# Fox prompt scores from two matmul passes: a stacked key and query pair, and the decay rows beside the key's low part

## The reference

```python
lk = jnp.cumsum(logf_all, axis=1)
lq = lk[:, Tk - T:]
s = jnp.einsum('bqhd,bkhd->bhqk', qi, k) * scale      # scale = 64 ** -0.5
s = s + (lq[t] - lk[s])                                # per head, per (t, s)
s = jnp.where(k_pos[None, :] <= pi[:, None], s, -jnp.inf)
p = jax.nn.softmax(s, axis=-1)
o = jnp.einsum('bhqk,bkhd->bqhd', p, v)
```

## Time and profile before

| | |
|---|---|
| median of the runs | 2846.46 us |
| span of the profiled execution | 2846.8 us |
| TensorE busy, whole span | 2649.1 us (93%) |
| VectorE, ScalarE, GpSimd busy | 938.1, 658.4, 437.9 us |
| mean granted clock of TensorE | 0.958 |
| fox, first score to last exponential | 1685.8 to 1857.7 us |

### The profile page before, as it was taken

How to read it: one execution, slowest core, us unless ns; L and a number is a source line. 1 busy time by engine, 2 the same in 40 slices (tenths; PEclk the granted TensorE clock), 3 DMA queues, 4 the chain that set the end, 5 groups by cost and what they waited for, 6 DMA issues and landing times. The chain is left out here.

```text
span 2846.8 us, 35924 instructions
## 1 busy us (share of the span) xinstructions
PE 2649.1 (93%) x14251; PEld 2340.2 (82%) x14251; DVE 938.1 (33%) x1612; ACT 658.4 (23%) x1138; POOL 437.9 (15%) x229
## 2 busy tenths in 40 slices
PE   5999999999996997889889969989899999999997
PEld 5999999999995887768745448867899999999996
DVE  4222222222226222554422254434222222222224
ACT  4111111111124011434222214433311111111112
POOL 1111111111113000000000001022111111111112
PEclk8999999999998998989989979989899999999999
DMA  4111111111014221100133030022211111111103
GB/s 152 45 44 44 44 44 44 44 44 44 15 63 156 78 80 39 38 9 0 54 116 115 31 119 0 0 94 92 81 45 44 44 44 44 36 38 44 44 15 141
DMA packets 134646, 161.61 MB, mean 57 GB/s; under 512 B 9648, under 2 KB 105008, under 8 KB 132528
## 3 DMA queue, kind: packets, MB, share of 16 engines
q1 hardware_dynamic: 134576, 160.66, 17.5%
HBM read 138.04 MB, written 22.60 MB: 56 GB/s over the span
## 5 line engine op out<-in xcount | busy, mean ns | idle before, releaser
L65 PE MATMUL ffn_gate_ps<-all_xT_hi,ffn_gu_hi 128*128 128x384 f32 x1056 | 355.8, 337 | 20.4 <-DVE all_xT_lo L163 12.2
L378 DVE TENSOR_TENSOR ffn_prod<-ffn_up_ps,ffn_silu 128x384 f32<-128x384 f32 x132 | 73.6, 558 | 893.2 <-ACT ffn_silu L346 893.2
L66 PE MATMUL ffn_gate_ps<-all_xT_lo,ffn_gu_hi 128*128 128x384 f32 x1056 | 354.9, 336 | 0.0
L67 PE MATMUL ffn_gate_ps<-all_xT_hi,ffn_gu_lo 128*128 128x384 f32 x1056 | 354.9, 336 | 0.0
L65 PE MATMUL ffn_up_ps<-all_xT_hi,ffn_gu_hi 128*128 128x384 f32 x1056 | 352.9, 334 | 0.0
L67 PE MATMUL ffn_up_ps<-all_xT_hi,ffn_gu_lo 128*128 128x384 f32 x1056 | 352.7, 334 | 0.0
L66 PE MATMUL ffn_up_ps<-all_xT_lo,ffn_gu_hi 128*128 128x384 f32 x1056 | 352.7, 334 | 0.0
L346 ACT ACTIVATE ffn_silu<-ffn_gate_ps 128x384 f32<-128x384 f32 x132 | 64.9, 492 | 1222.3 <-PE ffn_up_ps L67 1222.3
L65 PE MATMUL ffn_down_ps<-ffn_dn_hi,ffn_a_hi 128*128 128x512 f32 x792 | 309.2, 390 | 2.2 <-DVE all_acc L391 2.1
L391 DVE TENSOR_TENSOR all_acc<-ffn_down_ps,all_acc 128x512 f32<-128x512 f32 x360 | 246.0, 690 | 195.1 <-PE ffn_down_ps L67 195.1
L67 PE MATMUL ffn_down_ps<-ffn_dn_hi,ffn_a_lo 128*128 128x512 f32 x792 | 308.6, 390 | 0.0
(11 more groups left out here) (348 smaller groups left out, 3947.7 us busy)
## 6 DMA issues: line engine op xcount, KB each, us to landing
gu_raw<-in_w_ffn_gu SPq DMA_DIRECT2D x88, 512.0 KB, 5.1
ffn_dn_raw<-in_w_ffn_down SPq DMA_DIRECT2D x22, 1024.0 KB, 4.9
h<-all_acc SPq DMA_DIRECT2D x18, 512.0 KB, 2.9
dec_high_fk<-in_cache_fox_k SPq DMA_DIRECT2D x8, 1024.0 KB, 5.3
dec_x_fv<-in_cache_fox_v SPq DMA_DIRECT2D x8, 1024.0 KB, 4.7
out_fox<-inp_stage SPq DMA_DIRECT2D x27, 256.0 KB, 2.0
in_raw<-in_w_in SPq DMA_DIRECT2D x6, 1024.0 KB, 7.5
fox_x_rows<-out_fox SPq DMA_DIRECT2D x3, 2048.0 KB, 14.8
```

Of the source, the lines that this page charges most:

```text
L65: pe.matmul(out, w_hi, x_hi, start=first, stop=False)
L66: pe.matmul(out, w_hi, x_lo, start=False, stop=False)
L67: return pe.matmul(out, w_lo, x_hi, start=False, stop=last)
L378: dve.tensor_tensor(prod[:, u % 2, :], up_ps[:, u % 2, 0:GN], silu[:, u % 2, :], ALU.mult).then_inc(prod_ok, 1)
```

## The change

Only the fox stage takes it (`stacked=True`); the mla stage keeps its three passes.

- The products of the 64 head columns of high with high and high with low become one pass over 128 partitions. `k_twice` holds the key's high part twice, `q_both` holds the query's high part on partitions 0 to 63 and its low part on 64 to 127.
- The second pass is `kT_lo` against `qT_hi` on 104 partitions. kT_lo holds the key's low part and, on 64 to 75, the decay rows; qT_hi holds the high part, the low maxima on 64 to 71, the decay rows on 72 to 75 and the high maxima on 96.
- q_st and k_st are 76 wide: eight columns of zeros (q) and ones (k) at 64 leave room for the low maxima.
- ScalarE writes, for each half of k and ahead of the high part, the upper half of k_twice and the decay rows of kT_lo.
- GpSimd writes the lower halves of k_twice (an add with zero) and q_both (a copy), behind its v copy; TensorE waits for that on `doubled`. GpSimd also waits for VectorE's clearing before it stages the first head.
- VectorE clears with three memsets a buffer pair where there were five.

```diff
-        CLEARS = 2 * 2
+        doubled = k.sem("doubled")
+        CLEARS = 9 if stacked else 4
+        ROWS_CLEARED = 2 if stacked else 4
...
+                    if stacked:
+                        pool.memset(q_st[b][:, :, 64:64 + PT], 0.0).then_inc(cleared, 1)
+                        pool.memset(k_st[b][:, :, 64:64 + PT], 1.0).then_inc(cleared, 1)
+                if stacked:
+                    pool.memset(zero[:, :], 0.0).then_inc(cleared, 1)
+                    pool.wait_ge(cleared, CLEARS)
+                    pool.wait_ge(rows_cleared, 2 * ROWS_CLEARED)
...
                         pool.tensor_copy(v_st[b][:, :, 0:VD], v_of(i * 2 + b)).then_inc(v_staged, 1)
+                        for h in range(HALVES if stacked else 0):
+                            cols = slice(h * HALF, h * HALF + HALF)
+                            pool.wait_ge(prep_hi, i * (2 * PREP) + (b * PREP + 2 * h + 2))
+                            pool.tensor_tensor(k_twice[b][0:64, cols], plain(kT_hi[b][0:64, cols]), zero[0:64, :].broadcast_to([64, HALF]), ALU.add).then_inc(doubled, 1)
+                            pool.tensor_copy(q_both[b][0:64, cols], plain(qT_hi[b][0:64, cols])).then_inc(doubled, 1)
...
                         act.wait_ge(prepared, n * PREP + (2 * PREP + r + 1))
+                        if stacked and r % 2:
+                            act.activation(k_twice[b][64:P, r // 2 * HALF:r // 2 * HALF + HALF], turn[0:64, r % 2, :], ACT.Copy)
+                            act.activation(kT_lo[b][64:kdim, r // 2 * HALF:r // 2 * HALF + HALF], turn[64:kdim, r % 2, :], ACT.Copy)
                         act.activation(hi, turn[0:kdim, r % 2, :], ACT.Copy, scale=scale if r % 2 == 0 else 1.0).then_inc(prep_hi, 1)
...
-                        dve.scalar_tensor_tensor(lo, turn[0:kdim, r % 2, :], scale if r % 2 == 0 else 1.0, plain(hi), ALU.mult, ALU.subtract).then_inc(turn_out[r % 2], 1)
+                        rows = 64 if stacked else kdim
+                        dve.scalar_tensor_tensor(lo, turn[0:rows, r % 2, :], scale if r % 2 == 0 else 1.0, plain(hi[0:rows, :]), ALU.mult, ALU.subtract).then_inc(turn_out[r % 2], 1)
...
+                def clear_stacked(b):
+                    dve.memset(plain(qT_hi[b][64:KROWS, :]), 0.0).then_inc(rows_cleared, 1)
+                    dve.memset(plain(kT_lo[b][64:NM, :]), 0.0)
+                    dve.memset(plain(kT_lo[b][NM:KROWS, :]), 1.0).then_inc(rows_cleared, 1)
...
                         pe.wait_ge(turn_out[h % 2], n * PASS + (1 + PASS))
+                        if stacked:
+                            pe.wait_ge(doubled, n * DOUBLES + (h + 1) * DOUBLES // 2)
...
-                    last = split_product(pe, scores[:, s % 2, 0:w], kT_hi[b][:, t * P:t * P + P], kT_lo[b][:, t * P:t * P + P],
-                                         qT_hi[b][:, c0:c0 + w], qT_lo[b][:, c0:c0 + w], True, not diagonal)
+                    if stacked:
+                        pe.matmul(scores[:, s % 2, 0:w], k_twice[b][:, t * P:t * P + P], q_both[b][:, c0:c0 + w], start=True, stop=False)
+                        last = pe.matmul(scores[:, s % 2, 0:w], kT_lo[b][:, t * P:t * P + P], qT_hi[b][:, c0:c0 + w], start=False, stop=not diagonal)
+                    else:
+                        last = split_product(pe, scores[:, s % 2, 0:w], kT_hi[b][:, t * P:t * P + P], kT_lo[b][:, t * P:t * P + P],
+                                             qT_hi[b][:, c0:c0 + w], qT_lo[b][:, c0:c0 + w], True, not diagonal)
```

More of the change, by code:

```diff
@@ L819, in prompt_attention @@
         qT_hi = [k.sb(f"qT_hi{b}", [KROWS, SEQ], F32R) for b in range(2)]
-        qT_lo = [k.sb(f"qT_lo{b}", [KROWS, SEQ], F32R) for b in range(2)]
         kT_hi = [k.sb(f"kT_hi{b}", [KROWS, SEQ], F32R) for b in range(2)]
         kT_lo = [k.sb(f"kT_lo{b}", [KROWS, SEQ], F32R) for b in range(2)]
+        if stacked:
+            q_both = [k.sb(f"q_both{b}", [P, SEQ], F32R) for b in range(2)]
+            k_twice = [k.sb(f"k_twice{b}", [P, SEQ], F32R) for b in range(2)]
+            zero = k.sb("zero", [P, 1])
+        else:
+            qT_lo = [k.sb(f"qT_lo{b}", [KROWS, SEQ], F32R) for b in range(2)]
         nmax = [k.sb(f"nmax{b}", [P, PT, PT]) for b in range(2)]
@@ L845, in prompt_attention @@
         o_taken = k.sem("o_taken")
-        CLEARS = 2 * 2
+        doubled = k.sem("doubled")
+        CLEARS = 9 if stacked else 4
+        ROWS_CLEARED = 2 if stacked else 4
         def prep_parts(b, r):
-            st, hi, lo = (q_st, qT_hi, qT_lo) if r % 2 == 0 else (k_st, kT_hi, kT_lo)
             cols = slice(r // 2 * HALF, r // 2 * HALF + HALF)
-            return st[b], hi[b][0:kdim, cols], lo[b][0:kdim, cols]
+            if stacked:
+                st, hi, lo = (q_st, qT_hi, q_both[b][64:P, cols]) if r % 2 == 0 else (k_st, kT_hi, kT_lo[b][0:64, cols])
+            else:
+                st, hi, lo = (q_st, qT_hi, qT_lo[b][0:kdim, cols]) if r % 2 == 0 else (k_st, kT_hi, kT_lo[b][0:kdim, cols])
+            return st[b], hi[b][0:kdim, cols], lo
         with k.block() as block:
@@ L928, in preparation @@
                         dve.wait_ge(maxima_hi, n * HALVES + (g + 1))
-                        dve.tensor_tensor(qT_lo[b][NM:KROWS, cols], turn[0:PT, g % 2, :], plain(qT_hi[b][NM:KROWS, cols]), ALU.subtract).then_inc(turn_out[g % 2], 1)
+                        maxima_lo = qT_hi[b][64:64 + PT, cols] if stacked else qT_lo[b][NM:KROWS, cols]
+                        dve.tensor_tensor(maxima_lo, turn[0:PT, g % 2, :], plain(qT_hi[b][NM:KROWS, cols]), ALU.subtract).then_inc(turn_out[g % 2], 1)
                 def normalise(n, b, h):
@@ L957, in _ @@
                 clear(1)
-                dve.wait_ge(rows_cleared, 8)
+                dve.wait_ge(rows_cleared, 2 * ROWS_CLEARED)
                 dve.wait_ge(cleared, CLEARS)
@@ L1040, in _ @@
                 pe.wait_ge(cleared, CLEARS)
-                pe.wait_ge(rows_cleared, 4)
+                pe.wait_ge(rows_cleared, ROWS_CLEARED)
                 for step in range(NCH):
@@ L1112, in stage @@
             pool.tensor_copy(q_st[:, :, 0:64], rows[0][:, :, bass.ds(n * 64, 64)]).then_inc(done, 1)
-            pool.tensor_copy(q_st[:, :, 64:66].unsqueeze(2), q_decay[:, :, bass.ds(n, 1), :]).then_inc(done, 1)
-            pool.memset(q_st[:, :, 66:68], 1 / scale).then_inc(done, 1)
+            pool.tensor_copy(q_st[:, :, 72:74].unsqueeze(2), q_decay[:, :, bass.ds(n, 1), :]).then_inc(done, 1)
+            pool.memset(q_st[:, :, 74:76], 1 / scale).then_inc(done, 1)
             pool.tensor_copy(k_st[:, :, 0:64], rows[1][:, :, bass.ds(n * 64, 64)]).then_inc(done, 1)
-            pool.memset(k_st[:, :, 64:66], 1.0).then_inc(done, 1)
-            pool.tensor_copy(k_st[:, :, 66:68].unsqueeze(2), k_decay[:, :, bass.ds(n, 1), :]).then_inc(done, 1)
+            pool.memset(k_st[:, :, 72:74], 1.0).then_inc(done, 1)
+            pool.tensor_copy(k_st[:, :, 74:76].unsqueeze(2), k_decay[:, :, bass.ds(n, 1), :]).then_inc(done, 1)
         def v_of(n):
             return rows[2][:, :, bass.ds(n * VD, VD)]
-        prompt_attention(nc, "fox", ident, ident_bf, mask_bf, 68, scale, loaded, 3, stage, 6, v_of, o_rows, H * VD, load_next)
+        prompt_attention(nc, "fox", ident, ident_bf, mask_bf, 64 + PT + 4, scale, loaded, 3, stage, 6, v_of, o_rows, H * VD, load_next, stacked=True)
 NEW = DECT
```

11 lines of the change are left out of this document (7 added, 4 removed).

## The result

| | before | after |
|---|---|---|
| median of 6 runs each | 2851.58 us (2845.43 to 2855.30) | 2950.47 us (2932.03 to 2953.68) |
| profiled execution, span | 2846.8 us | 2948.4 us |
| mean granted clock | 0.958 | 0.921 |

The ratio is 1.0345, with a 95% interval of 1.0328 to 1.0361: 3.4% slower, where no change was forecast. A pass per chunk is gone, and the kernel loses some 99 us.

What follows compares the result with a forecast made beforehand. Took TensorE to bound fox, except where the transposes–ScalarE–VectorE chain ends last in seven heads. Passes -17.3, chain +14.0, tile 4 +1.5, start +1.3 sum to -0.5 us: 2846.0 us, 8-in-10 range 2837 to 2856.

Steps and rivals of the forecast that it cites:

- the passes: Fox scores: one of three passes removed in each of 96 chunks, 2.16 us a head, 17.3 us saved.
- the sum of that case: Rival in fox's preparation: ScalarE's copies cost the chain nothing, 13.6 us faster, 2832.5 us; chance 0.07.
- the place and size of the gaps: TensorE in seven heads: new 1.1 us gap before r3 transposes; gap before first rough product from 0.85 to 1.8.
- the next thing that is late: Fox, tile 4's rough product, released by VectorE's maxima: can move by 0.22, not 0.44; 1.5 us lost.
- the sum: Whole kernel: -17.3 + 14.0 + 1.5 + 1.3 = -0.5 us against before, giving 2846.0 us.
- the copies' spacing: ScalarE ahead of k's high parts: 0.50 us for each copy, four a head; bounds 0 and 0.59.
- the start: Start of fox: GpSimd waits for VectorE's memsets before staging, first rough product 1.3 us later; bounds -1 and 2.7.
- GpSimd is off the path: GpSimd's added copies and adds, 2.4 to 6.1 us a head; TensorE's wait for `doubled` taken at nothing.
- the rival in which GpSimd holds VectorE up: GpSimd's adds cannot run beside VectorE's low parts: 17 us on the chain, 2863 us; chance 0.05.
- The clock falls: Rival: TensorE's clock drops at the second gap in 7 heads, at least 10.5 us, 2856.5 us; chance 0.09.
- Three us of matmul work in each of 7 heads: Matmul work behind the second gap assumed to run at 1.2 GHz in the clock rival; at least 10.5 us.
- my upper end of 2856: Whole kernel: top of the 8-in-10 range 2837 to 2856, reaching to the clock's case.

Runs made afterwards that it cites:

- e2: Changed kernel with ScalarE's four copies a head moved behind the preparation, read from kT_hi; 2833.83 us, ratio 0.9943 to the kernel before.
- e3: Changed kernel with eight 512-column matmuls, results overwritten, ahead of the wait for the first rough product; 2849.18 us, ratio 1.0011 to the kernel before.
- e6: Changed kernel with five 512-column matmuls ahead of the r3 transposes, the second gap left unfilled; 2954.06 us, ratio 1.0361 to the kernel before.
- e1: Kernel before, three passes kept, with two extra ScalarE copies per k half that nothing reads; 2981.97 us, ratio 1.0477 to the kernel before.
- e5: Changed kernel with ten 512-column, 76-row matmuls ahead of tile 5's rough product, behind the gaps; 2968.19 us, ratio 1.0415 to the kernel before.
- e7: Changed kernel with ScalarE's copies off the chain and no GpSimd wait for VectorE's memsets before staging the first head; 2829.25 us, ratio 0.9926 to before.
- e4: Changed kernel with only kT_lo's ScalarE copy moved off the chain, k_twice's left on it; 2899.30 us, ratio 1.0170 to the kernel before.
- e9: Changed kernel with twenty 128x128 transposes ahead of tile 5's rough product, behind the gaps; 2896.62 us, ratio 1.0174 to the kernel before.
- e10: Changed kernel with twenty 512-column, 128-row matmuls ahead of tile 5's rough product, behind the gaps; 2911.94 us, ratio 1.0222 to the kernel before.

## Why the prediction was wrong

**Right: the passes.** 17.3 us was their worth; e2, with the clock held and the copies off the chain, is 12.4 faster (its interval is 10.5 to 21.9) where the sum of that case was 13.6. (The 2832.5 that the prediction gives for it should be 2832.9.)

**Right: the place and size of the gaps.** 1.1 and 1.8 us were forecast, 1.14 (e3) and 1.86 measured, both released by VectorE's low part of k.

**Right: the next thing that is late.** In e3 tile 4's product comes 3.11 us behind the head's first, for 3.33 before: 0.22 earlier, as forecast. With it, the rest of the head from the first rough product on is 1.53 us shorter, where the sum had 1.74 - 0.22 = 1.52.

**Mis-sized, small: the copies' spacing.** I took 0.50 from the earlier trace rows, where each high part waits for its own transposes; the three ScalarE instructions in a row start 0.60 apart, each 0.59 long, the upper bound. Four copies at 0.10 more are 0.4 us a head; e3's head takes 22.56 for 22.16 before, and the sum had +0.06 (-2.16 + 2.0 + 0.22). The difference is 0.34, all of it ahead of the first rough product (7.61 us behind chunk 1's scores, where the sum had 7.27); times 7 it is 2.4 us, which with -0.5 and the start below comes near e3's measured +3.0.

**Mis-sized, small: the start.** Two executions can be some us apart before fox begins, so I count from the stage's first memset (1657.38 in before, 1657.58 in after). GpSimd staged 6.95 us behind it (forecast 6.4), the first transposes came at 8.70 (forecast 8.0), and the first rough product at 16.91 (forecast 16.2, before 14.97): 1.9 us later for 1.3. Part of it is that the transposes came 1.75 behind the start of the staging for the 1.46 taken.

**Right: GpSimd is off the path.** Its timeline in after, and VectorE's at the same moment:

```profile
1728.73 1.03 POOL L895 TENSOR_TENSOR fox_k_twice<-fox_kT_hi,fox_zero 64x512 fp32r<-64x512 f32 x1 [3.52 <-ACT fox_kT_hi L913]
1729.71 0.60 POOL L896 CAST fox_q_both<-fox_qT_hi 64x512 fp32r<-64x512 f32 x1
...
1728.68 0.68 DVE L946 SCALAR_TENSOR_TENSOR fox_kT_lo<-fox_turn,fox_kT_hi 64x512 fp32r<-64x512 f32 x1 [1.16 <-ACT fox_kT_hi L913]
```

The low part takes 0.68 beside the add, for 0.67 alone: the rival in which GpSimd holds VectorE up is refuted. The wait for `doubled` released TensorE nowhere.

**The step that failed: the rival "The clock falls".** The sum ran at a clock of 1.00 throughout and left the loss of it to this rival. The rival named this mechanism and this place, and failed twice. First in its chance of 0.09. I set one row against it: a gap of 2.48 us behind which the transposes were fast. That row is sound (the clock there is 1.00 in before and in after), but it is one gap in another pattern of work, and I let it stand for a rule that a gap's length decides. The runs show that length alone does not: 1.73 lost the clock in fox (e6), 2.48 kept it there, and within fox 1.26 lost it (e1) where 1.90 kept it (e5). No row of before had a gap over 0.85 in a steady head of fox. The same ffn stage had a bound on the other side, a gap of 4.01 us in which the clock fell to 0.50 (at about 879.7):

```profile
882.40 1.97 PE L198 MATMUL ffn_up_ps<-all_ident,ffn_exit_normed 128*128 128x128 f32 x8 [4.01 <-DVE ffn_exit_normed L175]
...
879.80:885.00 5.20, 1.97 (x8) 1.57 (x8) 5.20 (x11) 3.56 (x10) 3.33 (x1) 0.50 0.56 202
```

The new gap of 1.8 lies between the 0.85 that fox had and these, so the chance could not rest on the convenient row alone. The Trainium skill (TensorE: Matmul & The Clock Gate, HAM oscillation), which has idle gaps between bursts throttle TensorE, named the kind of loss that happened; its own case is one of DMA waits, longer than fox's gaps.

Second in its price. "Three us of matmul work in each of 7 heads" at the low clock gave 10.5 us; it was the least price, and I made it the case's time. Measured, the clock stays low until the next head's preparation: 27 us and more at half speed, 12 to 13 us a head. A head took 34.9 for e3's 22.56, 12.3 more, times the 6 stretches between the seven first rough products is 74; from the seventh to the last scores after took 49.5 (1907.30 to 1956.8) and e3 27.2 (1827.20 to 1854.4), 22 more. That makes 96, and the ratios of after and e3 are 95 us apart.

What before's trace shows of the way back to full clock would have misled too. At the start of fox it came back 3.7 us behind the last gap, which ended at 1684.97:

```profile
1685.00:1688.60 3.60, 3.60 (x13) 2.19 (x14) 1.37 (x2) 1.22 (x3) 0.00 (x0) 0.50 0.00 0
1688.70:1690.00 1.30, 1.30 (x14) 1.30 (x13) 0.10 (x1) 1.17 (x3) 0.00 (x0) 1.00 0.00 0
```

That is close to the three us assumed, and in a steady head it took 27 to 37 us (after, e1). No row of before had a clock lost inside a head, so the honest price ran from 10.5 to all work up to the stage's next change of pattern, that is half of each head's 20 busy us and more, over 70 us; my upper end of 2856 came from the lower one.

## What to carry to other kernels

Before a copy goes ahead of the instruction that a chain waits for, price the gap that it opens on TensorE twice: as idle time, and as a possible drop of the clock over all the work that follows until the clock returns. Put such copies behind the chain (e2, e7), or, where they can't move, fill the gap with matmuls whose results are thrown away (e3): 1.8 us of them saved some 14 us a head here. A removed matmul is worth its time only if the engine is kept at full clock, so read the granted clock of the changed stage before any other row.

## What the runs showed of the hardware

- Among fox's matmuls single gaps up to 1.15 us (e3) never cost TensorE's clock; single gaps of 1.73 us cost it in seven heads of seven (e6). In between, and once above, it went both ways: lost at 1.26 and 1.62 (e1), kept at 1.27 and 1.45 (e4) and 1.90 (e5). Two gaps in one preparation cost it in 36 of 36 heads, the smallest pairs being 0.54 with 1.13 and 0.36 with 1.27 (e4). A gap of 2.48 in the ffn kept it. What decides is open.
- The fall is not tied to the gap's end: in after it comes 0.1 to 2.2 us behind it, in e9 and e10 in several heads up to 1.2 us ahead of it, within the second gap (in e9 the clock is at 0.50 from 1751.4, the gap ends at 1752.05).
- At 0.50, TensorE can be busy without a pause for 27 to 31 us (between two preparations of after) or 49 us (its last head) and not get the clock back. 4.3 us of 76-row matmuls, 512 columns each, did not bring it back either (six heads of six that had lost it); in seven heads of seven twenty transposes of 128 columns did within 1.2 to 4.5 us of their start, and so did twenty 128-row matmuls.
- ScalarE's copies of 12 and of 64 partitions by 512 columns take the same 0.59 us, and in a row they do not overlap (0.60 apart).
- GpSimd adds 64x512 in 1.03 us and copies it in 0.60, and VectorE is not slowed beside it where one of its operands comes from PSUM (0.68 for 0.67).
